# Neighbourhood attention with three units in flight, and side work placed anew, in a two-block kernel

## The chip, the cores and the metric

The kernel runs on one core of a Trainium2 chip. The metric is the device time of one execution in microseconds (us); lower is better. The core's engines run side by side, each with its own list of instructions, and wait for each other by semaphores: TensorE (PE: matrix products and transposes), VectorE (DVE), ScalarE (ACT), GpSimd (POOL), and SyncE (SP), whose queue here only starts DMA transfers. PE writes to PSUM, which has eight banks; DVE and ACT carry the results on to SBUF.

## The reference

A sequence of 512 tokens of width 1024 (and 256 context tokens) goes through two blocks. Block one has a gated linear attention layer ("A") and a dilated attention layer ("B", six heads h = 0 to 5, three groups each). Block two has two layers, l = 0 and l = 1; l = 0 updates the context too. The lines that matter, cut from `_layer`:

```python
shift, scale, gate = jnp.split((jax.nn.silu(c) @ w_mod + b_mod)[:, None, :], 3, axis=-1)
na_k, na_v, df_k, df_v, na_q, na_g, df_q, df_g, cv_a, cv_b, cv_g = _split_cols(h @ w_in, len(COL_SPLITS))
a_out = _neighbourhood_attention(...)   # 6 heads of 64: a local window with bias, and 256 context keys, one softmax
b_out = _diff_merge(_diff_attend(...))  # (softmax(q1 k1^T) - lam * softmax(q2 k2^T)) v, 4 heads; sub-layer norm weights
c_out = _conformer_conv(cv_a, cv_b, conv_w, conv_b, ln_g, ln_b)   # 31 taps over positions, LayerNorm, swish
y = jnp.concatenate([a_out * jax.nn.silu(na_g), b_out * jax.nn.silu(df_g), c_out * jax.nn.silu(cv_g)], axis=-1) @ w_out
x_new = x + gate * _rms(y, g_post)
```

## The kernel before

`schedule()` writes one list of steps. PE, DVE and ACT each walk that same list in its order and do their share of every step. A step that writes to PSUM has one job per bank, and a letter for who empties it ("a" ACT, "v" DVE); a job's `claim` on PE waits until the last job that held its bank has been emptied. An engine's instructions stay in the order of the list, so what ACT or DVE does late for one step delays all their later steps.

The projections multiply in split precision. Each weight chunk is rounded to a high part on ACT (`split hi`, L1399) and the rest is made from it on DVE (L1853) or, for early chunks, on POOL (L1303); `head_split(n)` says which. `Bproj h g` are the projections of head h in layer B, `BS`, `BT`, `BPV` its scores, transposes and products with the values, and `Bw` the weights of its three groups. For `Bw` small statistics (`stat`) go out to DRAM (`st_dram`) and back by SP's queue (L1210, L1214). Between these steps stand 16 pieces of the modulation of block two: `mod` (16 products on PE, L2403, with 1.5 MB of `w_mod` from one DMA, L1169) and `modC`, a small one behind it. SP's queue takes its transfers in order of due step, one list for all: `w_mod`, statistics, weight chunks.

In block two each layer has:

- **neighbourhood attention**, 12 units (n, j), each with two PSUM banks: `nS` (scores on PE, L2321; the maximum and bias on DVE, L2175 and L2178; exp on ACT, L1665), `nW` (DVE divides by the sum, L2187 and L1755), `nT` (eight transposes on PE, L2378, copied by ACT and by DVE, L2196) and `nPV` (product with the values, L2699, bank 6). Before, l = 0 has two units in flight (banks 0 to 3) and l = 1 three (banks 0 to 5). Between them stand the eight `gate` projections (24 products of 128x512 each) and, for l = 0, eight `gatec` (256 columns): work that PE has at hand. Each is emptied by ACT through silu (L1542, L1544), and gates 3 to 5 are then scaled on DVE by the weights of the sub-layer norm (L1755 `subw`).
- **convolution taps** (L1776, 31 for each of two feature blocks, on DVE alone), spread in portions over `nq`, the neighbourhood and the `dF k` steps; `cvT` transposes their result on PE, `cvZ` transposes back and puts it through silu on ACT (L1718).
- **differential attention**: `dF` projections, `dP`/`dX` (rope, transposes), `dv` (values), and then per item `dS` (scores; maximum on DVE L2230, exp on ACT L1703), `dT`, `dPV`.

## Time and profile before

| | |
|---|---|
| three runs | 1841.69, 1847.93, 1852.33 us; median 1847.93 |
| profiled execution | 1851.54 us, its span 1849.7 us |
| PE busy | 1692.6 us, 92% of the span |
| DVE busy | 951.9 us, 51% |
| ACT busy | 669.6 us, 36% |
| POOL busy | 221.0 us, 12% |

All times in the text are microseconds from the start of the span. A row of waits names an engine's line and what it waited for; a row of windows gives the busy time of every engine in a stretch and PEclk, the share of full TensorE clock that was granted there, which is 2.4 GHz at 1.00 and 1.2 GHz at 0.50. So PE's busy time multiplied by PEclk is what the same work takes at full clock, and a stretch less that is what waits and lower clock cost together.

### The profile page before, as it was taken

Reading aid. Unit: us, or ns where it says so; the run is one execution under the profiler, and the core shown is the slowest. Engines: PE = TensorE matmul, PEld = TensorE weight load, DVE = VectorE, ACT = ScalarE, POOL = GpSimd, SP = SyncE. Lnnn points to the kernel's source line nnn. Section 1 sums busy time; section 2 is a strip of 40 time slices with the busy share of each in tenths; the row PEclk is TensorE's granted clock in tenths of the full one; section 3 lists DMA queues with packets and bytes.
Section 4 is the critical chain, followed back from the end, with each engine's and each line's share of the span. In section 5 each row is a group of like instructions: output and inputs, shape, how many; then the busy total and the mean of one; then the engine's idle time right before and its main releaser. Section 6 shows DMA issues by size and latency. Waiting matters only on the chain.

```text
span 1849.7 us, 22824 instructions
## 1 busy us (share of the span) xinstructions
PE 1692.6 (92%) x8922; PEld 1319.2 (71%) x8922; DVE 951.9 (51%) x1662; ACT 669.6 (36%) x1249; POOL 221.0 (12%) x230
## 2 busy tenths in 40 slices
PE   7999977988999999979998899979989978987897
PEld 6866756876888888868887678845548866776553
DVE  1233263255656566465277766446654565563462
ACT  3254442333223323343215543334433245323341
POOL 3044223230000000121001100001110000000000
PEclk9998988999999999989999999979999989997699
DMA  7211042324564755333141120320012321221000
GB/s 261 69 35 58 23 182 85 103 73 115 166 173 103 171 146 141 126 114 109 42 147 41 52 69 1 118 98 1 12 44 87 120 74 52 69 91 69 1 12 35
DMA packets 170834, 161.34 MB, mean 87 GB/s; under 512 B 39958, under 2 KB 153864, under 8 KB 170696
## 3 DMA queue, kind: packets, MB, share of 16 engines
q1 hardware_dynamic: 167592, 150.04, 26.7%
q0 software_dynamic: 2848, 9.74, 1.4%
q8 instruction: 72, 1.18, 0.3%
q14 instruction: 34, 0.28, 0.1%
q10 hardware_dynamic: 288, 0.10, 0.0%
HBM read 149.80 MB, written 11.18 MB: 87 GB/s over the span
## 4 chain that ended last, share of the span: by engine, by line
PE 79%; DVE 12%; ACT 3%; issue 3%; DMA 1%; POOL 1%; ACTq 0%; SPq 0%; DVEq 0%; POOLq 0%
PE psum L2350 43%; PE psum L2321 12%; PE psum L2378 7%; PE psum L2808 6%; PE psum L2369 4%; PE psum L2479 2%; PE psum L2422 2%; DVE arena L1776 1%; DVE stat L2230 1%; PE psum L2403 1%; PE psum L2699 1%; DVE wring_r L1853 1%; DVE arena L1755 1%; DVE wring_r L1859 1%; DVE hT L1792 1%
## 5 line engine op out<-in xcount | busy, mean ns | idle before, releaser
L2350 PE MATMUL psum<-hT_r,wring_r 128*128 128x512 f32 (+1 forms) x1768 | 593.1, 394 | 0.0
L2350 PEld LDWEIGHTS psum<-hT_r,wring_r 128*128 128x128 f32 (+1 forms) x1768 | 330.8, 187 | 81.0 <-issue 8.6
L2350 PE MATMUL psum<-arena_r,wring_r 128*128 128x256 f32 (+2 forms) x1416 | 382.1, 337 | 1.8 <-DVE arena_r L1899 1.8
L1399 ACT ACTIVATE arena<-psum 128x512 f32<-128x512 f32 (+5 forms) x247 | 147.4, 620 | 504.3 <-PE psum L2350 289.2
L2321 PE MATMUL psum<-arena 128*128 128x96 f32 (+9 forms) x1460 | 240.0, 393 | 22.1 <-ACT arena L1399 11.3
L2350 PEld LDWEIGHTS psum<-arena_r,wring_r 128*128 128x128 f32 (+1 forms) x1416 | 229.0, 191 | 32.1 <-issue 4.2
L2321 PEld LDWEIGHTS psum<-arena 128*128 128x128 f32 (+5 forms) x1460 | 172.9, 205 | 85.7 <-issue 48.4
L2378 PE MATMUL psum<-ident,arena 128*128 128x128 f32 (+2 forms) x1028 | 145.4, 295 | 76.0 <-DVE arena L1755 42.7
L2350 PE MATMUL psum<-arena_r 128*128 128x512 f32 (+2 forms) x680 | 211.0, 351 | 0.0
L2378 PEld LDWEIGHTS psum<-ident,arena 128*128 128x128 f32 (+2 forms) x1028 | 126.1, 152 | 97.1 <-DVE arena L1755 47.1
L2350 PE MATMUL psum<-hT_r,arena_r 128*128 128x512 f32 (+1 forms) x408 | 163.7, 401 | 6.0 <-POOL wring_r L1303 6.0
L2350 PEld LDWEIGHTS psum<-arena_r 128*128 128x128 f32 (+1 forms) x680 | 120.9, 191 | 17.1 <-issue 0.3
L2808 PE MATMUL psum<-wring,branch 128*128 128x512 f32 x256 | 119.7, 614 | 4.9 <-issue 4.9
L1776 DVE SCALAR_TENSOR_TENSOR arena<-arena,vec 128x783 f32<-128x783 f32 (+1 forms) x120 | 108.7, 906 | 3.1
L1853 DVE SCALAR_TENSOR_TENSOR wring_r<-wring,wring_r 128x1024 fp32r<-128x1024 f32 x61 | 77.4, 1292 | 52.2 <-ACT wring_r L1399 52.0
L1399 ACT ACTIVATE wring_r<-wring 128x1024 fp32r<-128x1024 f32 (+1 forms) x87 | 88.5, 1040 | 43.2 <-DMA wring<-in_w_in 18.8
L2350 PEld LDWEIGHTS psum<-hT_r,arena_r 128*128 128x128 f32 (+1 forms) x408 | 77.8, 191 | 28.2 <-POOL wring_r L1303 6.7
L2230 DVE TENSOR_REDUCE stat<-psum 128x2 f32<-128x1536 f32 x32 | 56.2, 1757 | 80.3 <-PE psum L2321 80.3
L2808 PEld LDWEIGHTS psum<-wring,branch 128*128 128x128 f32 x256 | 47.6, 195 | 66.8 <-issue 66.8
L1399 ACT ACTIVATE arena_r<-wring 128x1024 fp32r<-128x1024 f32 (+3 forms) x74 | 77.7, 1083 | 11.9 <-DMA wring<-in_w_out 5.5
L2028 DVE LOAD_MASK_SELECT arena<-arena x18 | 0.3, 14 | 144.9 <-ACT arena L1399 144.9
L1703 ACT ACTIVATE hT<-psum,stat 128x768 f32<-128x768 f32 (+1 forms) x54 | 43.0, 802 | 73.8 <-DVE stat L1755 73.8
(221 smaller groups left out, 2059.0 us busy)
## 6 DMA issues: line engine op xcount, KB each, us to landing
wring<-in_w_in_b SPq DMA_DIRECT2D x54, 512.0 KB, 5.9
arena<-in_w_mod SPq DMA_DIRECT2D x16, 1536.0 KB, 10.1
wring<-in_w_in SPq DMA_DIRECT2D x16, 1536.0 KB, 6.9
wring<-in_w_out SPq DMA_DIRECT2D x8, 2048.0 KB, 10.8
wring<-in_w_in_a SPq DMA_DIRECT2D x5, 1536.0 KB, 6.5
arena<-x_dram SPq DMA_DIRECT2D x3, 2048.0 KB, 13.4
wring<-in_w_in SPq DMA_DIRECT2D x6, 1024.0 KB, 5.5
arena<-ebias_dram SPq DMA_DIRECT2D x144, 32.0 KB, 1.8
```

Of the source, the lines that this page charges most:

```text
L1399: return nc.scalar.activation(out, in_, ACT.Copy, scale=scale)
L1703: free(nc.scalar.activation(dst, src, ACT.Exp, bias=d_neg[:, n % 4, half:half + 1], scale=diff_scale, accum_out=d_s[:, n % 4, half:half + 1]))
L1776: ins_ = nc.vector.scalar_tensor_tensor(dst, src, w, dst, ALU.mult, ALU.add)
L1853: nc.vector.scalar_tensor_tensor(rest, w, 1.0, hi.bitcast(F32), ALU.mult, ALU.subtract).then_inc(head_lo, 1)
L2230: chained(nc.vector.reduce_max(d_max[:, p], psum[:, 0:4, 0:KEYS // 2].rearrange("p (s b) k -> p s b k", s=2), AX_XY))
L2321: ins_ = nc.tensor.matmul(out, lhsT, rhs, start=i == 0, stop=i == len(pairs) - 1)
L2350: ins_ = nc.tensor.matmul(b[0:hi.shape[2], 0:width], w[:, k], v[:, k], start=k + p == 0, stop=(k, p) == (KT - 1, 2))
L2369: ins_ = nc.tensor.matmul(out, v, w, start=i + p == 0, stop=(i, p) == (KT - 1, 2))
L2378: return nc.tensor.transpose(out, in_, ident[0:n, 0:n])
L2422: ins_ = nc.tensor.matmul(banks[g], w[:, k], v[:, k], start=k + p == 0, stop=(k, p) == (KT - 1, 2))
L2479: ins_ = nc.tensor.matmul(b[:, 0:384], v, w[:, 0:384], start=k + p == 0, stop=(k, p) == (KT - 1, 2))
L2808: ins_ = nc.tensor.matmul(psum[:, 7], src[:, k, tt * P:(tt + 1) * P], w[:, k], start=k == 0, stop=k == 5)
```

## The change

1. Modulation: no piece after `BS` of head 0, one more after `gate B 7` at the end; every piece moves one slot later. The first statistics go to SP's queue ahead of the second `w_mod`. `head_split` gives the rests of nine early weight chunks (Bproj 0) to DVE instead of POOL.
2. Neighbourhood: three units in flight in both layers. The work of DVE and ACT on the scores is a step of its own (`nM`, `nE`), placed with unit u for unit u + 2. All gates go through bank 7 (before, for l = 0, banks 4, 5 and 7). In l = 1 each gate comes in two halves (`gatep`, `gate`), one with each unit. The rounding of weights now stands behind `nE`.
3. The scaling of gates 3 to 5 is a step `subs` in the `dF k` steps. Taps: l = 0 has 6, 6, 0 in `nq` (before 5, 5, 5), l = 1 one with each unit, 12 instead of 7.
4. `cvT` stands two projections earlier; `cvZ` goes from behind `dF v 1` to behind the second `dS`; the first `dS` stands ahead of `dv`. `dv`, `cvZ` and two `dX` use banks 4 to 7 only.

```diff
@@ schedule @@
         add("aaavvvv", "BS", h)
-        modulation()
+        if h:
+            modulation()
...
             add("a", "gate", "B", 7)
+            modulation()
             add("avav", "BT", h)
...
             add(*keys[p])
+            add("", "subs", l, p)
             add("", "taps", l, ("k", p), 4 if both else 7)
...
         turn(0)
+        add("v" * (2 + both), "cvT", l)
         add(*queries[1])
         turn(1)
         add(*queries[2])
         turn(2)
-        add("v" * (2 + both), "cvT", l)
...
-        add("aa" * (1 + both), "cvZ", l)
         turn(4)
         add(*values[2])
         turn(5)
-        for t in range(TT + CT):
-            add("av"[t % 2], "dv", l, t)
-        turn(6)
-        diff_stage(add, l)
+
+        def between():
+            for t in range(TT + CT):
+                add("av"[t % 2], "dv", l, t)
+            turn(6)
+
+        def then():
+            add("aa" * (1 + both), "cvZ", l)
+
+        diff_stage(add, l, between, then)
...
@@ neighbourhood(add, l), new @@
+    filled(2)
+    for u in range(DEPTH):
+        add("aa", "nS", l, *units[u])
+        if u < 2:
+            softmax(u)
+            filled(1)
     add("", "nW", l, *units[0])
     for u, unit in enumerate(units):
+        if l == 0 and u:
+            product(u - 1)
         add("av", "nT", l, *unit)
         if u + 1 < len(units):
             add("", "nW", l, *units[u + 1])
+        softmax(u + 2)
+        if l and u:
+            product(u - 1)
+        filled(1)
+        add("", "taps", l, ("n", u), 2 - l)
+        if u + DEPTH < len(units):
+            add("aa", "nS", l, *units[u + DEPTH])
+    product(len(units) - 1)
...
@@ diff_stage @@
         if n < len(items):
             add("aa", "dS", l, *items[n])
+        if n < 2:
+            (between, then)[n]()
...
@@ banks, in hybrid_stack_kernel @@
-            free_ = (7,) if key[0] == "gate" and key[1] == "C1" else (4, 5, 7) if key[0] in ("gate", "gatec") and key[1] == "C0" else range(BANKS)
+            free_ = (7,) if key[0] in ("gate", "gatec") and key[1][0] == "C" else range(4, BANKS) if late(key) else range(BANKS)
...
         def head_split(n):
-            return n >= before_mem
+            return n >= split_at[("Bproj", 0, 0), 0]
...
-                items.append((order_of[mod_key(3 * h)] + 0.5, "stats", h))
+                items.append((order_of[mod_key(3 * h - 1) if h else ("BS", 0)] + 0.5, "stats", h))
```

In the lists below a line number of the changed kernel stands for the same operation as one about 30 lines earlier in the kernel before (L1887 for L1853, L1789 for L1755, L1810 for L1776, L2226 for L2196, L2351 for L2321, L2409 for L2378).

DVE's list before, at one unit of the neighbourhood of l = 0 (from the copy of one unit's transposes to the maximum of the next scores):

```order
L2196 COPY arena<-psum 128x512 [waits psum_full]
L1752 TENSOR_TENSOR branch<-psum,branch 128x24x16 [waits evac_scalar,psum_full]
L1853 SCALAR_TENSOR_TENSOR wring_r<-wring,wring_r 128x8x128 [waits split_hi]
L1755 TENSOR_SCALAR branch<-branch,subw 128x512 [waits evac_scalar]
L2187 RECIPROCAL stat<-stat 128x2 [waits evac_scalar]
L1755 TENSOR_SCALAR arena<-arena,stat 128x512 [waits dve_chain]
L1755 TENSOR_SCALAR arena<-arena,stat 128x512
L1776 SCALAR_TENSOR_TENSOR arena<-arena,vec 128x783
L1776 SCALAR_TENSOR_TENSOR arena<-arena,vec 128x783 [waits dve_chain]
L2175 TENSOR_REDUCE stat<-psum 128x2 [waits psum_full,bias_ready,dve_chain]
```

DVE's list of the changed kernel, at one unit of the same stage:

```order
L2226 COPY arena<-psum 128x512 [waits psum_full,dve_chain]
L2217 RECIPROCAL stat<-stat 128x2 [waits evac_scalar]
L1789 TENSOR_SCALAR arena<-arena,stat 128x512 [waits dve_chain]
L1789 TENSOR_SCALAR arena<-arena,stat 128x512
L2205 TENSOR_REDUCE stat<-psum 128x2 [waits psum_full,bias_ready]
L2208 ISA psum,stat<-psum,arena,stat 128x256 [waits dve_chain]
...
L1789 TENSOR_SCALAR stat<-stat 128x2 [waits dve_chain]
L1887 SCALAR_TENSOR_TENSOR wring_r<-wring,wring_r 128x8x128 [waits split_hi]
L1810 SCALAR_TENSOR_TENSOR arena<-arena,vec 128x783
```

The scaling by `subw`, which waited for ACT's silu, has gone from between the copy and the division; the division, the maximum and its negative follow the copy at once, and the rest of the weights (`wring_r`, which waits for `split_hi` from ACT) stands behind them where it stood ahead.

PE's list before, where the differential attention of l = 1 begins: the last transposes of `dX`, six `dv` of three products each, the first two `dS` (four rows of 128x384 products), and the transposes of `dT` (from `hT`):

```order
L2378 MATMUL psum<-ident,arena 128x128 [waits evac_scalar,diff_staged]
L2378 MATMUL psum<-ident,arena 128x128 x3
L2378 MATMUL psum<-ident,arena 128x128 [waits evac_scalar,evac_vector]
L2378 MATMUL psum<-ident,arena 128x128 x2
...
L2378 MATMUL psum<-ident,arena 128x128 [waits evac_vector,evac_scalar]
L2378 MATMUL psum<-ident,arena 128x128 x2
L2321 MATMUL psum<-arena 128x384 [waits evac_scalar,evac_vector]
L2321 MATMUL psum<-arena 128x384 x3
L2321 MATMUL psum<-arena 128x384 [waits evac_scalar]
L2321 MATMUL psum<-arena 128x384 x3
L2378 MATMUL psum<-ident,hT 128x128 [waits evac_scalar,diff_w]
L2378 MATMUL psum<-ident,hT 128x128 x5
```

PE's list of the changed kernel at the same place:

```order
L2409 MATMUL psum<-ident,arena 128x128 [waits evac_vector,diff_staged]
L2409 MATMUL psum<-ident,arena 128x128 x3
L2351 MATMUL psum<-arena 128x384 [waits evac_scalar,evac_vector]
L2351 MATMUL psum<-arena 128x384 x3
L2409 MATMUL psum<-ident,arena 128x128 [waits evac_scalar,evac_vector]
...
L2351 MATMUL psum<-arena 128x384 [waits evac_scalar]
L2351 MATMUL psum<-arena 128x384 x3
L2409 MATMUL psum<-ident,arena 128x128 [waits evac_scalar,evac_vector]
L2409 MATMUL psum<-ident,arena 128x128 x3
L2409 MATMUL psum<-ident,arena 128x128 [waits evac_vector]
L2409 MATMUL psum<-ident,arena 128x128 x3
L2409 MATMUL psum<-ident,hT 128x128 [waits evac_scalar,diff_w]
```

The first `dS` now stands ahead of the six `dv`, and the eight transposes of `cvZ` (4 and 4) between the second `dS` and the first `dT`.

SP's list before, at the end of layer B (the last chunks of w_out, then the statistics of head 5):

```order
L1161 DMA wring<-in_w_in_b 128x8x384 [waits psum_full]
L1169 DMA arena<-in_w_mod 128x8x384 [waits psum_full] x2
L1161 DMA wring<-in_w_out 128x8x512 [waits psum_full] x2
L1210 DMA st_dram<-stat 128x8x1 [waits dil_probs]
L1210 DMA st_dram<-stat 128x2x4 x2
L1214 DMA stat<-st_dram 128x2x4 [waits st_saved]
L1214 DMA stat<-st_dram 128x8x1 x2
```

SP's list of the changed kernel at the same place:

```order
L1194 DMA wring<-in_w_in_b 128x8x384 [waits psum_full]
L1202 DMA arena<-in_w_mod 128x8x384 [waits psum_full] x2
L1194 DMA wring<-in_w_out 128x8x512 [waits psum_full] x2
L1202 DMA arena<-in_w_mod 128x8x384 [waits psum_full]
L1243 DMA st_dram<-stat 128x8x1 [waits dil_probs]
L1243 DMA st_dram<-stat 128x2x4 x2
```

One transfer of `w_mod` now stands between the chunks of w_out and the statistics.

## Rows read from the trace of the kernel before

**Rows 1.** The page: PE's busy time, and the chain that ended last

```profile
PE 1692.6 (92%) x8922; PEld 1319.2 (71%) x8922; DVE 951.9 (51%) x1662; ACT 669.6 (36%) x1249; POOL 221.0 (12%) x230
...
PE 79%; DVE 12%; ACT 3%; issue 3%; DMA 1%; POOL 1%; ACTq 0%; SPq 0%; DVEq 0%; POOLq 0%
```

**Rows 2.** Waits of PE over the span: us in total, times, longest

```profile
PE psum L2378 <- DVE arena L1755: 42.7, 12, 10.3
PE psum L2378 <- DVE hT L1792: 12.4, 9, 3.5
...
PE psum L2321 <- ACT arena L1399: 11.3, 8, 2.4
...
PE psum L2321 <- ACT hT L1703: 8.0, 2, 5.5
...
PE psum L2350 <- POOL wring_r L1303: 6.0, 2, 3.6
PE psum L2403 <- issue: 5.1, 1, 5.1
```

**Rows 3.** Busy time by stretch: stretch, PE, PEld, DVE, ACT, POOL, PEclk, DMA

```profile
363.00:434.00 71.00, 65.01 (x302) 51.91 (x300) 41.31 (x55) 23.53 (x48) 18.35 (x7) 0.95 0.33 87
...
975.00:1103.00 128.00, 112.01 (x772) 91.61 (x772) 89.51 (x170) 70.07 (x109) 10.85 (x6) 0.95 0.16 46
1487.00:1600.00 113.00, 91.98 (x581) 71.79 (x581) 67.19 (x151) 57.09 (x94) 8.39 (x6) 0.89 0.21 59
...
1103.00:1186.00 83.00, 83.00 (x518) 71.85 (x515) 44.64 (x86) 27.00 (x56) 2.69 (x6) 1.00 0.20 70
1186.00:1236.00 50.00, 39.12 (x190) 27.29 (x189) 26.11 (x67) 19.45 (x53) 1.20 (x2) 0.73 0.31 116
1671.00:1746.00 75.00, 60.29 (x261) 42.28 (x260) 33.79 (x57) 25.56 (x47) 1.20 (x2) 0.64 0.12 42
```

**Rows 4.** Groups of DVE with shapes, 975:1103: busy, mean ns, idle before

```profile
L1853 DVE SCALAR_TENSOR_TENSOR wring_r<-wring,wring_r 128x1024 fp32r<-128x1024 f32 x7 | 8.6, 1225 | 10.5 <-ACT wring_r L1399 10.5
```

**Rows 5.** Timeline of a unit of l = 0: start, length, engine, idle before

```profile
1037.67 1.28 ACT L1544 ACT_TABLE_LOAD   x1
...
1038.96 0.38 ACT L1544 ACTIVATE arena<-psum 128x256 f32<-128x256 f32 x1
...
1039.38 0.35 DVE L1755 TENSOR_SCALAR arena<-arena,subw 128x256 f32<-128x256 f32 x1 [3.11 <-ACT arena L1544]
...
1040.78 1.09 PE L2378 MATMUL psum<-ident,arena 128*128 128x128 f32 x8 [1.94 <-DVE arena L1755]
```

**Rows 6.** Timeline of PE, the convolution's transposes in l = 1

```profile
1642.92 1.69 PE L2378 MATMUL psum<-ident,arena 128*128 128x128 f32 x14
1649.43 1.97 PE L2378 MATMUL psum<-ident,arena 128*128 128x128 f32 x8 [4.82 <-DVE arena L1776]
```

**Rows 7.** Timeline of DVE at the same place

```profile
1646.26 3.11 DVE L1776 SCALAR_TENSOR_TENSOR arena<-arena,vec 128x512 f32<-128x512 f32 x4
```

**Rows 8.** Timeline of POOL, rests of Bproj 0

```profile
376.59 9.03 POOL L1303 TENSOR_TENSOR wring_r<-wring,wring_r 128x1024 fp32r<-128x1024 f32 x3
```

**Rows 9.** Timelines of SP's queue and PE: w_mod transfers, modulation products

```profile
429.32 0.74 SPq L1169 DMA_DIRECT2D arena<-in_w_mod  x1
...
439.20 2.79 PE L2403 MATMUL psum<-arena,siluc 128*32 128x384 f32 x16 [5.14 <-issue]
...
766.28 1.50 PE L2403 MATMUL psum<-arena,siluc 128*32 128x384 f32 x16
```

**Rows 10.** Timelines of SP's queue and DVE, end of layer B

```profile
757.85 0.99 SPq L1161 DMA_DIRECT2D wring<-in_w_out  x2
772.15 1.51 SPq L1210 DMA_DIRECT2D st_dram<-stat  x3
...
787.02 0.17 DVE L2069 TENSOR_TENSOR stat<-stat 128x8 f32<-128x8 f32 x1 [7.05 <-DMA stat<-st_dram]
```

**Rows 11.** Timeline of ACT, silu of the convolution in l = 0

```profile
1186.52 2.36 ACT L1718 ACTIVATE arena<-psum,vec 128x512 f32<-128x512 f32 x4 [1.41 <-PE psum L2378]
```

More of the change, by code:

```diff
@@ L301, in schedule @@
                 end -= 1
-            while split < min(n + units - (key[0] in ("Bproj", "BS") or key[0] == "hcT"), end):
+            while split < min(n + units - (key[0] in ("Bproj", "BS") or key[0] == "hcT") + (key[0] == "nq") - (key[:2] == ("gate", "C1")), end):
                 out.append((("split", split), ""))
@@ L343, in neighbour_units, with product, softmax, late @@
     return [(n, j) for n in range(NQB) for j in range(NH // 2)]
[L346 to L348 removed]
 def neighbourhood(add, l):
[L354 to L356 removed]
+    units = neighbour_units()
+    gates = [step for i in range(KT) for step in ((("a", "gate", "C0", i), ("a", "gatec", "C0", i)) if l == 0 else
+                                                  (("", "gatep", "C1", i), ("a", "gate", "C1", i)))]
     def filled(n):
         for _ in range(n):
[L361 to L363 removed]
+            add(*gates.pop(0))
+    def product(u):
+        n, j = units[u]
+        add("v" * (j == NH // 2 - 1), "nPV", l, n, j)
+    def softmax(u):
+        if u < len(units):
+            add("", "nM", l, *units[u])
+            add("", "nE", l, *units[u])
+    filled(2)
+    for u in range(DEPTH):
         add("aa", "nS", l, *units[u])
[L365 removed]
+        if u < 2:
+            softmax(u)
+            filled(1)
     add("", "nW", l, *units[0])
     for u, unit in enumerate(units):
+        if l == 0 and u:
+            product(u - 1)
         add("av", "nT", l, *unit)
[L369 to L372 removed]
         if u + 1 < len(units):
             add("", "nW", l, *units[u + 1])
[L375 to L378 removed]
+        softmax(u + 2)
[6 more added lines that the diff above has]
+    product(len(units) - 1)
     assert not gates
+def late(key):
+    return key[0] == "dv" or key[0] == "cvZ" or key in (("dX", 0, "q", 2), ("dX", 0, "q", 3))
 def diff_tiles(l):
@@ L389, in diff_items, with diff_stage @@
     return [(t, h) for t in diff_tiles(l) for h in range(DH)]
-def diff_stage(add, l):
+def diff_stage(add, l, between, then):
     tiles, items = diff_tiles(l), diff_items(l)
@@ L478, in hybrid_stack_kernel @@
         readers += list(who)
-    ordinal, seen = [], {"a": 0, "v": 0}
-    for who in readers:
-        seen[who] += 1
-        ordinal.append(seen[who])
     njobs = {key: len(who) for key, who in steps}
+    ordinal, seen = [0] * len(readers), {"a": 0, "v": 0}
+    for key, _ in steps:
+        emptied = ("nS", *key[1:]) if key[0] == "nE" else key
+        if key[0] != "nS":
+            for n in range(base[emptied], base[emptied] + njobs[emptied]):
+                seen[readers[n]] += 1
+                ordinal[n] = seen[readers[n]]
     held, earlier, last_job = [], [], [-1 - i for i in reversed(range(BANKS))]
@@ L1664, in _ @@
                     for half in range(2):
-                        free(nc.scalar.activation(nprob[l][i % depth][:, half], bank(key, half), ACT.Exp,
-                                                  bias=n_neg[:, i % depth, half:half + 1],
-                                                  accum_out=n_s[:, i % depth, half:half + 1]))
+                        free(nc.scalar.activation(nprob[i % DEPTH][:, half], bank(scores, half), ACT.Exp,
+                                                  bias=n_neg[:, i % DEPTH, half:half + 1],
+                                                  accum_out=n_s[:, i % DEPTH, half:half + 1]))
                 elif kind == "nT":
@@ L2345, in split_features @@
                     evacuated(pe, ("hcT", key[1]), 3)
-                for k in range(KT):
+                for k in blocks:
                     if new and i == 0:
@@ L2426, in _ @@
                             turn_tokens(pe, ("hT", f"C{l}"), src, k + HT_BANKS)
+                elif kind == "gatep":
+                    split_features(("gate", *key[1:]), 0, 0, 0, range(KT // 2))
+                elif kind == "gate" and key[1] == "C1":
+                    split_features(key, 0, 0, 0, range(KT // 2, KT))
                 elif (split_jobs(key) and kind != "Aproj") or kind == "gatec":
```

83 lines of the change are left out of this document (33 added, 50 removed).

## The prediction, written before the changed kernel had run

> **What bounds the kernel now.** I read the page first. PE is busy for 92% of the span and makes 79% of the chain that ended last [rows 1]: the kernel goes at PE's pace, and time can come only from PE's waits and from the clock that it runs at. The waits of PE say where they are [rows 2]: 42.7 us in 12 waits for DVE's L1755, the scaling of probabilities, above all at `nT` of the neighbourhoods; then the differential attention (12.4 us for L1792, 8.0 for ACT's L1703), and single waits at rests from POOL (6.0 in two) and for w_mod (5.1). The windows by stretch give the sizes [rows 3]. In the neighbourhood of l = 0 (975 to 1103) PE is busy 112.0 of 128.0 us at a clock of 0.95: 112.0 x 0.95 = 106.4 us of work at full clock, so 21.6 are lost, 16.0 of them idle. In l = 1 (1487 to 1600) it is 92.0 of 113.0 at 0.89: 81.9 of work, 31.1 lost. In the `dF k` stretch (1103 to 1186) PE is busy all 83.0 us at 1.00 while DVE works only 44.6: DVE work is free there.
>
> The clock falls behind waits. In the stretch with no idle time it stays 1.00, in the two neighbourhoods 0.95 and 0.89, in the stretches that begin the differential attention 0.73 and 0.64 [rows 3]. The 16 modulation products that follow 5.14 us of idle took 2.79 us, the same 16 with PE busy before them 1.50 [rows 9]. A wait removed thus gives back more than itself, and I take it from these lost sums.
>
> **Part 2 and 3, neighbourhood of l = 0.** At a typical unit DVE stood 3.11 us for ACT's silu before it could scale a gate by `subw` (1039.38), the division of the probabilities came behind that, and PE waited 1.94 for it (1040.78) [rows 5]. DVE also stood 10.5 us in seven waits at a rest of the weights for ACT's high part, ahead of the division [rows 4]. The change takes both from between the copy and the division, and puts a third unit in flight, so that the softmax of u + 2 has a unit's time before `nT` needs it. What paces next? DVE is busy 89.5 us over 12 units [rows 3], 14.9 for a pair, less some 0.4 for the scalings that leave: 14.5. For PE I take 1.07 each for `nS`, `nT` and `nPV`, near the 1.09 of `nT` [rows 5], 3.2 a unit; the 16 gate pieces then have (106.4 - 38.4) / 16 = 4.25 each, and a pair of iterations, with two pieces, is 14.9. The two are level, so I allow 0.7 a pair for gates that find bank 7 not yet emptied, since ACT has two table loads of 1.28 a pair beside its exps: 15.6. Six pairs are 93.6. Ahead of the first `nT` stand four gate pieces (17.0) and three `nS` (3.2), 20.2 in all; the last three iterations have no `nS`, less 3.2. Sum 110.6, against 128.0: **-17**. From below, PE's work and nothing else (106.4) gives -21.6; from above, half of the waits stays: -11.
>
> **Part 2 and 3, l = 1.** The same with gates in halves. The tap work grows from 7 to 12, some 0.75 us each (four took 3.11) [rows 7]; DVE's 67.2 us [rows 3], less three scalings, is 10.9 a pair, 11.5 with the taps. PE's gates are (81.9 - 38.4) / 8 = 5.4, and its work of a pair 11.8. I choose 13.1 a pair, 1.3 above, for what DVE and ACT still expose: 78.6 for six. Ahead stand four half gates (10.9), and the first `nT` waits some 3.0, while DVE clears taps and a rest, with 2.5 of clock: 95.0, against 112.1 from its first to its last step: **-17**. Bounds: PE's work alone, 81.9, gives -31; half of the waits left gives -10. The lower bound is far, since here more is lost now; nearer to it I would need a pair without any wait.
>
> **Part 3 elsewhere.** The scalings, six and three operations of DVE, lie in the `dF k` steps, where DVE has 38 us to spare in l = 0 [rows 3]: 0. If that cover were gone they would cost some 2.5 us in l = 0, six at the 0.35 of a 128x256 one [rows 5] or a little more.
>
> **Part 4, cvT.** In l = 1 PE waited 4.82 us in the middle of `cvT` for the last taps, and the transposes behind it ran at a lower clock [rows 6]; DVE had four taps of 3.11 us in all still to do, behind the rope of `dP` [rows 7]. Twelve taps in the neighbourhood instead of seven make 62 of 62 done by `dF k 2`, before PE gets to `cvT`, though `cvT` stands earlier. The wait goes, 4.8, with some 2.2 of clock: **-7** (bounds -5 and -7). In l = 0 there is no such wait, before or after: 0.
>
> **Part 4, begin of the differential attention.** The first `dS` goes ahead of `dv` and starts its softmax earlier, but `dv` has only banks 4 to 7, so its fifth job waits for the copy of the first, which on ACT stands behind the exps of the first `dS`. And the silu of `cvZ`, in l = 0 2.36 us for four (1186.52) [rows 11] and one table load of 1.28 (as [rows 5] has it) each way, now stands on ACT between the second exps and the first copy of `dT`. What PE gains is that `cvZ`'s own transposes (1.3 and 0.9 us) lie under a wait. I get +2.6 - 1.3 = **+1.3** in l = 0, and **+1.4** in l = 1, at clocks of 0.73 and 0.64 [rows 3]. Bounds: all of the new order hidden, -3 each; the whole detour of ACT on the path at half clock, +5 each.
>
> **Part 1, modulation and rests.** At the start of layer B POOL took 9.03 us for three rests [rows 8], DVE takes 1.225 for one [rows 4]. PE's waits there are 6.0 in two, and the stretch 363 to 434 loses 71.0 - 65.0 x 0.95 = 9.2 us [rows 2, 3]. With DVE the first wait goes (-3.4 with its clock), a new one comes at the next projection, where the rest is queued behind DVE's copy for the projection before (1.9 taken, between nothing and the 3.4), and the wait of 3.6 shrinks to 2.4 (-1.2): -2.7. At 434 PE waited 5.14 for w_mod, issued at 429.32 and used at 439.20, and lost 6.5 with the clock [rows 9]. That wait goes; but the second w_mod is now queued behind the statistics of head 0 and, by the same 9.9 us from issue to use, comes some 2.3 us after PE gets to it: about 4.1 with clock. Net -2.4. At the end of B w_mod (1.5 MB) now lies between w_out and the statistics of head 5. Those were issued at 772.15, when the two w_out transfers had landed, and DVE had them at 787.02 after 7.05 us of idle, PE's `BT 5` waiting for it [rows 10]. In flight beside 1.5 MB the small transfers come 0.5 to 2.5 us later, and the extra `modC` pair stands between: **+2** (1 to 4). Part 1 in all: **-3**.
>
> **Sum.** -17 - 17 - 7 + 1.3 + 1.4 - 3 = -41. The profiled execution took 1851.5 us, 3.6 more than the median of the runs (1847.9). It would become 1810.5; a median over runs, 1807.
>
> **Rivals.** (a) *The chain through DVE and ACT paces on.* With one bank for all gates, each gate waits for ACT, which stands in exps and table loads. ACT works 70.1 us in l = 0 [rows 3], 5.8 a unit, and can't reorder. Then half of the neighbourhoods' loss stays: 1824. For it: DVE's 14.5 a pair is level with PE's 14.9. Against: both have slack of some 40 and 60 us in the stage before. Chance 0.2. The Trainium skill (ScalarE: Activation LUTs, What ACT_TABLE_LOAD costs) gives 1.28 us for the load and 1.38 more for a drain, 2.66 a switch. By that, an estimate, two switches a unit would add 2.8 us to each of ACT's units and bring case (a) about in l = 0. Here the load took 1.28 and the next activation began 1038.96, where the load ended [rows 5]; the drain is not seen, and it adds nothing to the chance.
> (b) *Slower.* Bank 7 makes the stage serial: a gate can't start until ACT has emptied the one before, ACT stands behind the exps of u + 2, these behind DVE's maximum, and that behind the scores which PE issues after the gate. A unit of l = 0 would be about 14.7 us (gate and gatec on average 4.3, `nS` and `nPV` 2.1, division, `nT`, copy, maximum, exps, silu with its loads 8.3) for 10.7 now, 48 us for twelve, with half of that in l = 1: 1890. It turns the sign from 13.4 a unit on. Against: the scores of u + 2 are issued a unit ahead. Chance 0.04, with 0.05 more that losses and gains cancel within 0.5%.
> (c) *More is gained.* PE has hardly a wait left, the clock stays at 1.00 in both neighbourhoods as it does in the `dF k` stretch, and the pairs go at PE's work, 106 and 87: 1793. Chance 0.11.
> (d) *The begin of the differential attention costs more*, 4 to 5 us a layer: 1814, inside my own range.
>
> **How the numbers follow.** The forecast with (d) has 0.6, its own range 1796 to 1818. (a) 0.2, (c) 0.11, no change 0.05, slower 0.04. Leaving out a tenth at either side, the range is 1790 to 1829. 0.5% is 9 us, about what a measurement of this kernel tells from no change: faster 0.91, same 0.05, slower 0.04.
>
> **What the profile after would show.** Right: PE's waits for L1755 (now L1789) fall from 42.7 to below 20; windows of the two neighbourhoods of about 111 and 95 us at a clock of 0.97 and more; no wait at `cvT` in l = 1; no wait of PE for POOL in B; one wait for w_mod at the second piece, smaller than 5.1. Wrong: PE waits at gates for ACT's silu, or for L1399 at `nS`; the first `dT` in either layer waits more than before; or the statistics of head 5 reach DVE more than 19 us after their issue (now 14.9).

## The result, and the profile after

The changed kernel takes 1829.11 us (median of four runs, 1826.59 to 1830.79) against 1848.14 of the kernel before (four runs); the ratio is 0.990, 95% interval 0.987 to 0.993. It is faster by 19 us where I had forecast 41, and the time lies 0.1 us above the range.

The page of the changed kernel, its busy times and the chain that ended last (before: [rows 1]):

```profile
PE 1685.2 (92%) x8922; PEld 1309.9 (72%) x8922; DVE 950.4 (52%) x1671; ACT 672.8 (37%) x1251; POOL 195.0 (11%) x221
...
PE 78%; DVE 11%; ACT 4%; issue 4%; DMA 1%; POOL 1%; ACTq 0%; DVEq 0%; POOLq 0%
```

Waits of PE over its span: us in total, times, longest (before: [rows 2]):

```profile
PE psum L2434 <- issue: 19.0, 7, 8.9
PE psum L2409 <- DVE arena L1789: 17.9, 3, 10.3
...
PE psum L2409 <- ACT arena L1752: 9.9, 2, 5.4
PE psum L2380 <- ACT branch L1575: 7.3, 6, 2.2
...
PE psum L2409 <- ACT arena L1432: 6.8, 2, 4.4
PE psum L2380 <- ACT arena L1577: 6.6, 6, 1.9
```

What was aimed at has gone: the waits for the scaling of probabilities fell from 42.7 us in 12 to 17.9 in 3 (two of the three, 15.1 us of it, lie outside the windows of the two neighbourhoods), and the waits for `hT` by the first `dS` of the differential attention (8.0) and for the last taps are no more in the list. Four new ones stand in their place: L2434, the modulation's products, which wait for w_mod seven times (19.0, before 5.1 in one); L1575 and L1577, silu of the gates in bank 7; L1752, silu of `cvZ`; and a copy by L1432 for `dv`.

The windows of the two neighbourhoods, each from its first step to its last, changed kernel (columns as in [rows 3]):

```profile
979.90:1096.70 116.80, 107.97 (x770) 88.67 (x770) 78.56 (x158) 71.54 (x109) 8.66 (x6) 0.99 0.18 51
1484.00:1581.70 97.70, 88.37 (x578) 67.04 (x576) 65.81 (x150) 53.58 (x91) 7.69 (x6) 0.95 0.22 61
```

and the same two stretches of the kernel before:

```profile
974.90:1102.80 127.90, 111.91 (x770) 91.53 (x772) 89.41 (x169) 70.07 (x109) 10.85 (x6) 0.95 0.16 46
1487.20:1599.20 112.00, 91.00 (x577) 71.14 (x577) 66.38 (x148) 57.09 (x94) 8.39 (x6) 0.89 0.20 56
```

l = 0 went from 127.9 to 116.8 and l = 1 from 112.0 to 97.7: -11.1 and -14.3, and the clock rose in both. To see the rest I laid the starts of PE's steps of both traces side by side; how much a stretch between two steps grew or shrank is its part:

| stretch of PE's steps | forecast | measured |
|---|---|---|
| ahead of layer B (untouched by the change) | 0 | -2.9 |
| start of layer B: Bproj 0 and the first two w_mod | -5.1 | -4.7 |
| heads 1 to 5 of layer B | 0 | +10.7 |
| its end, gate B 5 to the hT transposes of l = 0 | +2 | +2.0 |
| neighbourhood, l = 0 | -17 | -11.1 |
| `cvT` to the third tile of the differential attention, l = 0 | +1.3 | +2.9 |
| neighbourhood, l = 1 | -17 | -14.3 |
| `cvT` in l = 1 | -7 | -5.9 |
| from there to the third tile | +1.4 | +2.7 |
| sum | -41.4 | -20.6 (the spans differ by 20.8) |

The largest surprise is 10.7 us in the heads of layer B, 8.7 of them in head 3 alone.

Some of these parts vary from trace to trace without any edit. What stands ahead of layer B took 357.7 to 363.2 us in the twelve traces that can be read, so the -2.9 is no gain of the change. The stretch from `BS` of head 0 to `BS` of head 1 took 66.4 us in the changed kernel and 63.6 to 65.0 in the eight other kernels that place the pieces as it does, so the -4.7 is on the low side.

### The profile page after: what moved, and what is told of

Its sections match the earlier page's. It is cut to its first block, busy times and chain, and to the rows that moved or that the text cites. A ratio compares the mean times of both kernels' runs of the same rounds, so it can differ in the third digit from the quotient of the medians.

```text
span 1828.9 us, 22822 instructions
## 1 busy us (share of the span) xinstructions
PE 1685.2 (92%) x8922; PEld 1309.9 (72%) x8922; DVE 950.4 (52%) x1671; ACT 672.8 (37%) x1251; POOL 195.0 (11%) x221
## 4 chain that ended last, share of the span: by engine, by line
PE 78%; DVE 11%; ACT 4%; issue 4%; DMA 1%; POOL 1%; ACTq 0%; DVEq 0%; POOLq 0%
PE psum L2380 44%; PE psum L2351 11%; PE psum L2843 7%; PE psum L2409 6%; PE psum L2400 4%; PE psum L2514 2%; PE psum L2453 2%; PE psum L2434 1%; DVE stat L2260 1%; DVE arena L1810 1%; DVE wring_r L1887 1%; DVE arena L1789 1%; DVE wring_r L1893 1%; ACT arena L1699 1%; DVE psum L2208 1%
## 5 line engine op out<-in xcount | busy, mean ns | idle before, releaser
L1432 ACT ACTIVATE arena<-psum 128x512 f32<-128x512 f32 (+5 forms) x247 | 147.2, 619 | 479.4 <-PE psum L2380 254.6
L2351 PE MATMUL psum<-arena 128*128 128x96 f32 (+9 forms) x1460 | 235.7, 387 | 4.6 <-ACT arena L1432 2.2
L2351 PEld LDWEIGHTS psum<-arena 128*128 128x128 f32 (+5 forms) x1460 | 169.1, 201 | 68.2 <-issue 46.2
L2409 PE MATMUL psum<-ident,arena 128*128 128x128 f32 (+2 forms) x1028 | 143.5, 292 | 48.0 <-DVE arena L1789 17.9
L2409 PEld LDWEIGHTS psum<-ident,arena 128*128 128x128 f32 (+2 forms) x1028 | 124.3, 151 | 68.8 <-issue 20.1
L1887 DVE SCALAR_TENSOR_TENSOR wring_r<-wring,wring_r 128x1024 fp32r<-128x1024 f32 x68 | 85.1, 1278 | 76.7 <-ACT wring_r L1432 76.5
L1432 ACT ACTIVATE wring_r<-wring 128x1024 fp32r<-128x1024 f32 (+1 forms) x87 | 88.3, 1039 | 56.2 <-DMA wring<-in_w_in 19.2
L1810 DVE SCALAR_TENSOR_TENSOR arena<-arena,vec 128x783 f32<-128x783 f32 (+1 forms) x120 | 106.9, 891 | 2.9
L2380 PEld LDWEIGHTS psum<-hT_r,arena_r 128*128 128x128 f32 (+1 forms) x408 | 77.1, 189 | 30.7 <-issue 7.6
L1432 ACT ACTIVATE arena_r<-wring 128x1024 fp32r<-128x1024 f32 (+3 forms) x74 | 77.7, 1082 | 16.9 <-DMA wring<-in_w_in_b 6.2
L1887 DVE SCALAR_TENSOR_TENSOR wring_r<-wring,arena_r 128x1024 fp32r<-128x1024 f32 x49 | 62.7, 1302 | 14.0 <-ACT arena_r L1432 13.8
## 6 DMA issues: line engine op xcount, KB each, us to landing
arena<-x_dram SPq DMA_DIRECT2D x3, 2048.0 KB, 10.6
```

What stands on the lines that cost most here:

```text
L1432: return nc.scalar.activation(out, in_, ACT.Copy, scale=scale)
L1810: ins_ = nc.vector.scalar_tensor_tensor(dst, src, w, dst, ALU.mult, ALU.add)
L1887: nc.vector.scalar_tensor_tensor(rest, w, 1.0, hi.bitcast(F32), ALU.mult, ALU.subtract).then_inc(head_lo, 1)
L2351: ins_ = nc.tensor.matmul(out, lhsT, rhs, start=i == 0, stop=i == len(pairs) - 1)
L2380: ins_ = nc.tensor.matmul(b[0:hi.shape[2], 0:width], w[:, k], v[:, k], start=k + p == 0, stop=(k, p) == (KT - 1, 2))
L2409: return nc.tensor.transpose(out, in_, ident[0:n, 0:n])
```

## The experiments

Each kernel ran four times, except those of experiments 4 and 5 (once). "Less than the changed kernel" compares medians with 1829.11 us. The kernel before was timed anew beside each group of runs: 1848.62 us beside experiments 1, 2, 3 and 7, 1849.68 beside 6, 8, 9 and 11, 1848.56 beside 4, 5 and 10, against 1848.14 above. So such a difference is good to some 1.5 us, beside the spread of the runs themselves.

**1. `modT` later.** In head 3 of the changed kernel PE waits twice for w_mod (L2434). SP's queue there, then POOL's and two rows of PE:

```profile
622.91 12.51 SPq L1210 DMA_DIRECT2D ebias_dram<-rpb_dram  x16
635.46 0.45 SPq L1202 DMA_DIRECT2D arena<-in_w_mod  x1
636.26 10.31 SPq L1243 DMA_DIRECT2D st_dram<-stat  x3
658.40 1.50 SPq L1247 DMA_DIRECT2D stat<-st_dram  x3
659.94 2.74 SPq L1194 DMA_DIRECT2D wring<-in_w_in_b  x3
662.73 2.12 SPq L1202 DMA_DIRECT2D arena<-in_w_mod  x1
...
631.00 1.88 POOL L1322 DMA_DIRECT2D gate_dram<-stat  x2 [293.09 <-DVE stat L1786]
...
649.39 1.50 PE L2434 MATMUL psum<-arena,siluc 128*32 128x384 f32 x16 [1.31 <-issue]
...
672.84 2.79 PE L2434 MATMUL psum<-arena,siluc 128*32 128x384 f32 x16 [4.85 <-issue]
```

The same queue in the kernel before, and `modT`'s two transfers at 611.56, ahead of the head's bias writes (`ebias_dram`), w_mod and statistics:

```profile
629.72 12.26 SPq L1177 DMA_DIRECT2D ebias_dram<-rpb_dram  x16
642.32 0.38 SPq L1169 DMA_DIRECT2D arena<-in_w_mod  x1
642.76 3.92 SPq L1210 DMA_DIRECT2D st_dram<-stat  x3
657.76 2.17 SPq L1214 DMA_DIRECT2D stat<-st_dram  x3
659.98 2.92 SPq L1161 DMA_DIRECT2D wring<-in_w_in_b  x3
662.94 1.60 SPq L1169 DMA_DIRECT2D arena<-in_w_mod  x1
...
611.56 1.89 POOL L1289 DMA_DIRECT2D gate_dram<-stat  x2 [199.50 <-DVE stat L1752]
```

The statistics went out and were ready to be read back 15.0 us later (642.76 to 657.76); in the changed kernel it took 22.1 (636.26 to 658.40), and the next w_mod stands behind that. Most of the difference arises while SP still issues the three writes: 10.31 us instead of 3.92. The edit:

```diff
-            if j == MODS - 1:
-                add("", "modT", l)
+            if (l, j) in ((1, 1), (1, MODS - 1)):
+                add("", "modT", 0 if j == 1 else 1)
```

> The changed kernel with one step moved: `modT` of layer 0, which sends the modulation's gate vector to DRAM by two small transfers from POOL, stands two pieces later, behind the second modulation piece after it. Theory 1 (the small scattered writes at 631 us share the DMA engines with the bias writes, w_mod and the statistics of head 3, and hold w_mod up): PE's waits of 1.3 and 4.9 us for w_mod in head 3 go, the piece of layer B from BS 3 to BS 4 takes 65.2 us as before the change instead of 73.8, and the kernel 8 to 9 us less: about 1820.5. Theory 2 (SP's queue itself is too late, since PE now reaches the pieces some 7 us earlier against the bias writes that stand ahead of w_mod on it): the waits stay, time 1829 within 3.

Measured: 1818.52 us, 0.983 of before (0.981 to 0.985), 10.6 less than the changed kernel. Its SP queue and the window of head 3:

```profile
632.78 0.45 SPq L1202 DMA_DIRECT2D arena<-in_w_mod  x1
633.59 3.80 SPq L1243 DMA_DIRECT2D st_dram<-stat  x3
648.33 1.50 SPq L1247 DMA_DIRECT2D stat<-st_dram  x3
```

```profile
621.70:687.10 65.40, 65.22 (x365) 53.51 (x364) 38.49 (x78) 21.22 (x46) 1.88 (x2) 1.00 0.62 149
```

14.7 us from the writes to the reads, a head of 65.4 us instead of 73.8, and the clock at 1.00. SP's queue stands to PE as it did: w_mod is issued 11.1 us after the start of `BS 3` in both. The rival (a queue that is late by itself) falls, and of theory 1 so much is shown: the two writes delay the transfers beside them. That they do it in the DMA engines is not shown. All traces agree: with `modT` where the change put it, head 3 takes 71.4 to 73.8 us (five kernels), otherwise 65.2 to 66.3 (seven).

The gain fell 22 us short, and this step is the largest single part of that: 10.6 us by the medians, 8.4 in head 3 by the traces. Another 4.9 us by which this trace is shorter in layer B lie in the heads before and behind, which the edit doesn't reach.

**2. Modulation undone.**

```diff
-        if h:
-            modulation()
+        modulation()
...
             add("a", "gate", "B", 7)
-            modulation()
...
-                items.append((order_of[mod_key(3 * h - 1) if h else ("BS", 0)] + 0.5, "stats", h))
+                items.append((order_of[mod_key(3 * h)] + 0.5, "stats", h))
```

> The changed kernel with the modulation pieces and the statistics on SP's queue put back where they were before the change; POOL's nine rests stay on DVE. If the new places cost what the two traces show (head 3 +8.7 us, small waits in heads 2 and 4 +2, end of layer B +2, against -5 for the first piece), the kernel takes some 8 us less than the changed one: about 1821. If the placement is as good as I predicted (-0.4 net without the rests), it takes the same time, 1829, or a little more.

Measured: 1824.28 us, ratio 0.987 (0.985 to 0.989); 4.8 less than the changed kernel. That is between the two expectations (8 and 0). From layer B's start to the hT transposes of l = 0 its trace takes 0.6 us more than the kernel before, the changed kernel 7.9 more. So the new places cost as built, and the collision is the reason: with `modT` out of the way (experiment 1) the same places take 5.0 us less than before.

**3. Begin of the differential attention undone.**

```diff
         add(*values[1])
+        add("aa" * (1 + both), "cvZ", l)
         turn(4)
         add(*values[2])
         turn(5)
-        def between(): ...
-        def then(): ...
-        diff_stage(add, l, between, then)
+        for t in range(TT + CT):
+            add("av"[t % 2], "dv", l, t)
+        turn(6)
+        diff_stage(add, l)
```

> The changed kernel with the begin of the differential attention put back: `cvZ` behind the second value projection, `dv` and the last `dX` ahead of the first `dS`, all banks free to them. `cvT` stays early. My theory (`dv 4` waits in bank 4 for ACT's copy of `dv 0`, which stands behind the exps of the first `dS`, and the first `dT` for cvZ's silu): it takes 5.6 us less than the changed kernel (2.9 in l = 0, 2.7 in l = 1), about 1823.5. Rival (the half clock after this place has its own causes, and the new order costs nothing): 1829 within 2.

Measured: 1818.85 us, ratio 0.984 (0.981 to 0.986), 10.3 less than the changed kernel. By the stretches of the traces 3.3 us are of l = 0 and 3.9 of l = 1; the rest is of other places, above all of layer B, where this run's waits for w_mod were shorter (4.8 us), which the edit does not touch. My mechanism had two parts, so three more kernels take them apart. All are read in us from the start of `dF v 1` to the first `dS` of a later tile, `dS 0 0 0` in l = 0 and `dS 1 2 0` in l = 1, so that `cvZ`'s place is inside for all:

| kernel | l = 0 | l = 1 |
|---|---|---|
| before | 59.4 | 87.6 |
| changed | 62.4 | 91.5 |
| 3. begin undone | 59.1 | 87.6 |
| 4. only `cvZ` moved | 64.4 | 91.0 |
| 5. only `dv` moved | 58.4 | 87.8 |
| 6. `dv` readers exchanged | 62.0 | 89.7 |

This stretch varies too: the kernels of experiments 1 and 2, which are as the changed kernel here, took 62.7 and 64.2 us in l = 0 and 91.5 and 91.4 in l = 1; those of experiments 8 to 11, which are as kernel 3, took 59.2 to 60.3 and 85.5 to 88.7. So kernels of the same order differ by up to 3 us. Over all twelve traces those with `cvZ` moved lie at 61.9 to 64.4 and 89.6 to 91.5, the others at 58.4 to 60.3 and 85.5 to 88.7, and the groups don't overlap.

**4. Only `cvZ` moved,** with `dv` and two `dX` still in banks 4 to 7.

```diff
-        diff_stage(add, l, between, then)
+        between()
+        diff_stage(add, l, lambda: None, then)
```

> The changed kernel with `dv` and the last `dX` put back ahead of the first `dS`, while `cvZ` stays behind the second. Read from the start of `dF v 2` to the first `dS` of the next tile that runs at full clock (`dS 0 0 0` and `dS 1 2 0`), where the changed kernel took 52.5 and 81.6 us, diff_start_undone 47.9 and 76.9. If cvZ's silu on ACT ahead of the first `dT` is the larger part, most of the 4.6 and 4.7 us stays: 51 to 53 and 80 to 82. If `dv` behind the softmax is, 48 to 50 and 77 to 79.

**5. Only `dv` moved.**

```diff
         add(*values[1])
+        add("aa" * (1 + both), "cvZ", l)
...
         def then():
-            add("aa" * (1 + both), "cvZ", l)
+            pass
```

> The changed kernel with `cvZ` put back behind `dF v 1`, while the first `dS` stays ahead of `dv` and `dv` keeps banks 4 to 7. The same stretches. If `dv` behind the softmax costs time, they stay above 47.9 and 76.9 by 1 us or more; if issuing the first `dS` early is worth its 2 us and only cvZ's silu cost, they fall below these, to 46 and 75.

One run each: 1831.26 and 1822.59 us. The expectations counted the stretch from `dF v 2`: 54.6 and 81.1 us for only_cvz_moved, 47.2 and 77.1 for only_dv_moved. With `cvZ` moved the loss stays whole; with `dv` moved neither of the two cases came, the times are those of kernel 3. So `cvZ` behind the second `dS` makes the loss, and for the first `dS` ahead of `dv` neither gain nor loss is seen: 0.7 us less than kernel 3 in l = 0, 0.2 more in l = 1. PE in l = 1, only `cvZ` moved:

```profile
1666.93 2.93 PE L2352 MATMUL psum<-arena 48*128 48x384 f32 x8 [5.48 <-ACT hT L1738]
1669.79 1.78 PE L2410 MATMUL psum<-ident,arena 128*128 128x128 f32 x8
1676.80 1.51 PE L2410 MATMUL psum<-ident,hT 128*128 128x128 f32 x6 [5.23 <-ACT arena L1753]
```

only `dv` moved:

```profile
1660.59 1.51 PE L2410 MATMUL psum<-ident,arena 128*128 128x128 f32 x6 [4.40 <-ACT arena L1433]
1662.03 2.93 PE L2352 MATMUL psum<-arena 48*128 48x384 f32 x8
1668.50 1.54 PE L2410 MATMUL psum<-ident,hT 128*128 128x128 f32 x6 [3.54 <-DVE hT L1827]
```

With `dv` moved, the softmax of the first item is waited for at `dv 4` (4.40) where it was waited for at the second `dS` (5.48 above): the same wait, 1.1 us smaller, at another step. With `cvZ` moved, the first `dT` waits 5.23 for its silu and not 3.54 for the combined weights. ACT of the changed kernel at that place:

```profile
1671.55 0.90 ACT L1737 ACTIVATE hT<-psum,stat 128x768 f32<-128x768 f32 x1 [5.51 <-DVE stat L1789]
...
1673.44 1.28 ACT L1752 ACT_TABLE_LOAD   x1
1674.74 1.45 ACT L1752 ACTIVATE arena<-psum,vec 128x512 f32<-128x512 f32 x2
```

The silu of `cvZ` starts only after both exps and a table load and ends at 1676.2; the first `dT` takes bank 4, which it holds, at 1676.33.

**6. The readers of `dv` exchanged.**

```diff
-                add("av"[t % 2], "dv", l, t)
+                add("va"[t % 2], "dv", l, t)
...
-                elif kind == "dv" and key[2] % 2 == 0:
+                elif kind == "dv" and key[2] % 2:
```

> The changed kernel with the readers of the six `dv` banks exchanged: DVE copies the first, third and fifth, ACT the others. `dv 4` then waits in bank 4 for DVE's copy and not for ACT's, but DVE has the maximum of the first `dS` (1.8 us each in l = 1) ahead of it, and `dv 5` in bank 5 still waits for ACT behind the exps. Theory (a copy in bank 4 or 5 that stands behind the softmax on its engine is what holds PE): the wait moves from `dv 4` to `dv 5` and the time stays within 2 us of 1829. Rival (only ACT's copy of `dv 0` matters): 4 us in l = 1 and 2 in l = 0 go.

Measured: 1827.49 us, ratio 0.987 (0.985 to 0.989), 1.6 less than the changed kernel. PE waited 1.2 us at `dv 4` (DVE) and 2.6 at `dv 5` (ACT) in l = 1 instead of 4.4 at `dv 4`: the wait moved as the theory says.

**7. Silu ahead of the exps.**

```diff
-        softmax(u + 2)
         if l and u:
             product(u - 1)
         filled(1)
+        softmax(u + 2)
```

> The changed kernel with each gate's step of the neighbourhood ahead of the softmax steps of unit u + 2, so that ACT empties bank 7 before it does these exps. Theory: the waits of PE for silu in bank 7 (6.6 us in six in l = 0, 6.5 in five in l = 1) go, with their share of clock, and the kernel takes 8 to 14 us less: about 1818. Rival: the exps now wait for the gate's last product, and with them the `nT` of u + 2; then waits of `nT` for DVE come back and the time stays at 1829 or rises.

Measured: 1807.68 us (median of the three runs of 1805 to 1809), ratio 0.978 (0.976 to 0.980), 21.4 less than the changed kernel where 8 to 14 were expected. The fourth run, the one with the trace, took 5763 us, PE's products being some three times as long from start to end; why is not known. It is left out, and the next kernel shows the stage.

**8. Three edits together** (1, 3 and 7).

> The changed kernel with the three edits together: `modT` of layer 0 later, the begin of the differential attention as it was before the change, and the silu of the gates ahead of the exps. If each took its time from a place of its own, as the stages of the traces say (head 3 -8.4 us, the two begins -7.1, the two neighbourhoods what is left of the 21 us by which silu_before_exps was faster than the changed kernel), they add: about 1791, between 1787 and 1797. If the edits give the same time twice (SP's queue late again once PE is earlier), it stays above 1800. The neighbourhoods should show no wait of PE for silu in bank 7 and a clock of 1.00, which the single run of silu_before_exps left without a readable profile.

Measured: 1800.02 us, ratio 0.973 (0.971 to 0.975). The neighbourhoods from `gate C0 0` to the last `nPV`, and from `gate C1 0` to the last `nPV` of l = 1:

```profile
973.00:1080.80 107.80, 105.29 (x771) 87.40 (x770) 81.33 (x158) 70.95 (x109) 7.95 (x6) 1.00 0.19 55
1466.30:1554.30 88.00, 85.22 (x578) 65.00 (x576) 66.30 (x150) 56.33 (x93) 7.66 (x6) 0.98 0.23 68
```

and all waits of PE in the first and in the second of the two (L2371 is the line of the gate products, L2400 that of the transposes):

```profile
PE psum L2371 <- DVE arena L1780: 1.5, 1, 1.5
PE psum L2371 <- ACT branch L1566: 0.8, 1, 0.8
PE psum L2371 <- ACT arena L1568: 0.2, 1, 0.2
...
PE psum L2400 <- DVE arena L1780: 2.8, 1, 2.8
```

l = 0 takes 107.8 us instead of 116.8, l = 1 88.0 instead of 97.7. The exps, now later by a gate, hold nobody up. So each neighbourhood had 9 us left in ACT's order, in waits and in the clock behind them, and the rival of experiment 7 falls. The sum came out 9 us above my 1791: PE's waits for w_mod are back, 14.5 us in four with 10.2 at the end of layer B, and the layer takes 6.6 us more than in experiment 1. That part of the gain is given back there, in a layer that the other two edits don't touch.

**9. The last piece late.**

```diff
             add("a", "gate", "B", 5)
-            add("", "Bw", h)
-            modulation()
             add("a", "gate", "B", 6)
             add("a", "gate", "B", 7)
+            add("", "Bw", h)
             modulation()
             add("avav", "BT", h)
...
+        if h == BH - 1:
+            modulation()
         add("va", "BPV", h)
```

> The same as three_edits, with the end of layer B changed: the last w_mod is needed only after `gate B 7` (order: gate B 5, 6, 7, Bw, piece, `BT`, piece, `BPV`). Theory: PE's 8.9 us wait for w_mod behind the w_out transfers lies under two gates of 5.4 us, and the statistics of head 5, which come in the same microseconds, are hidden too: 5 to 7 us less than three_edits. Rival: w_mod and the statistics land together at the end of the gates, `BT 5` waits for the statistics instead, and nothing is gained (within 2).

Measured: 1796.34 us, ratio 0.971 (0.969 to 0.974), 3.7 less than three_edits on the same chip; the two intervals overlap, so by the times alone this gain is not certain. The queue and PE at the end of layer B:

```profile
760.29 0.37 SPq L1194 DMA_DIRECT2D arena<-in_w_mod  x1
764.61 1.62 SPq L1235 DMA_DIRECT2D st_dram<-stat  x3
777.37 1.50 SPq L1239 DMA_DIRECT2D stat<-st_dram  x3
...
777.27 1.50 PE L2426 MATMUL psum<-arena,siluc 128*32 128x384 f32 x16
785.05 3.17 PE L2401 MATMUL psum<-ident,arena 128*128 128x128 f32 x15 [6.28 <-DVE arena L1778]
```

The products wait no more for w_mod; `BT 5` waits 6.28 us for the statistics, as it did before the change. By the stage of the traces (`gate B 5` to `BPV 5`: 35.1 us in three_edits, 29.2 here) it saves 5.9 us, so the theory holds in its first half; that the statistics would be hidden too was wrong.

**10. Rests back on POOL,** in the kernel of 9.

```diff
-            return n >= split_at[("Bproj", 0, 0), 0]
+            return n >= before_mem
```

> The kernel of late_end_piece with the nine rests of Bproj 0 back on POOL. By the stages of seven traces the rests on DVE save 2.8 us at the first projection, cost 3.9 at the second and save 1.2 at the third, so nothing: 1796 within 2. By my prediction (-3.4, +1.9, -1.2) it is 2.7 us slower, about 1799.

Measured: 1792.56 us, ratio 0.970 (0.967 to 0.972). The intervals of 9 and 10 overlap, so the two can't be told apart; 2.7 us slower it is not. Against the kernel before, Bproj 0 is 1.6 us shorter in this trace, with the rests on the same engine; with DVE its three projections are -2.8, +3.9 and -1.2. Over all traces the engine makes no difference: from the first projection to `BS` of head 0 it is 64.5 to 66.1 us with POOL (three kernels) and 64.5 to 66.2 with DVE (nine).

**11. The neighbourhood alone.** The changed kernel with the edits of 2, 3 and 10, and

```diff
         turn(0)
-        add("v" * (2 + both), "cvT", l)
         add(*queries[1])
         turn(1)
         add(*queries[2])
         turn(2)
+        add("v" * (2 + both), "cvT", l)
```

> The kernel before with the neighbourhood part of the change alone (three units in flight, softmax and gates placed anew, taps and the sub-layer scaling moved); modulation, POOL's rests, `cvT`, `cvZ`, `dv` and the first `dS` are where they were. From the stages of the traces: -11 to -13 us in l = 0, -14 to -16 in l = 1, and part of the 5.9 at `cvT` (its last taps come earlier now) though `cvT` stands late: about 1817 to 1823 against 1848, so faster than the whole change. If the parts help each other, it is slower than the whole change, above 1829.

Measured: 1816.55 us, ratio 0.982 (0.980 to 0.984), 12.6 us faster than the whole change, so the parts don't help each other. -10.4 in l = 0, -14.5 in l = 1, and the full -5.9 at `cvT`, where it stood before: five more taps in the neighbourhood are enough, and the earlier place of `cvT` gives nothing.

## Why the prediction was wrong

**The sign and the places of the gain were right; two terms of the sum were not:** layer B (-3 forecast, +8.0 measured) and the neighbourhoods (-34 forecast, -25.4 measured). What the forecast says of the removed waits for L1755 was borne out: they fell below 20 us. The clock of 0.97 and more came in l = 0 (0.99), not in l = 1 (0.95). Of the signs that would show the forecast wrong two came: gates waited for ACT's silu, and the first `dT` waited longer (5.42 us for 3.51 in l = 1). The third did not: the statistics of head 5 reached DVE 15.3 us after their issue.

**Part 1, modulation: the step that failed.** I followed the pieces on SP's queue and PE at the two ends of layer B, and put heads 1 to 5 at nothing, without a reason but that every piece moves one slot later. They cost 10.7 us, 8.7 in head 3. What moved there with the piece was `modT`, whose two small writes from POOL went from 611 into the microseconds of bias writes, w_mod and statistics. Experiment 1 takes them out, and head 3 is back at 65.4; the other 2 us in the heads are waits for w_mod that differ from trace to trace. All transfers of a moved step count, those of POOL too; POOL's timeline of the kernel before has them at 611. And the slack was small: before, the w_mod issued at 662.94 took 9.7 us, and PE needed it at 673.04, 0.4 later.

**Part 1, its ends.** Start -4.7 for -5.1 was right by luck: the rests brought 0 where I had -2.7, as the new wait at the second projection costs 3.9 and not the 1.9 that I chose, with its clock. The first w_mod brought -6.7 for -6.5 and the second cost 4.0 for 4.1; the missing 2.1 are the pair of `mod` and `modC` that leaves this place for the end of the layer, which I counted only there. At the end +2.0 for +2 was luck as well: I kept `BT 5`'s wait and let the statistics come 0.5 to 2.5 us later, a term that no row shows; from issue to DVE they took 15.3 us for 14.9. What came instead was a wait of PE for w_mod of 8.89 us, and `BT 5`'s wait, 8.1 us with its clock, disappeared behind it. That w_mod took 15.0 us to land (770.82 to 785.79). The w_out transfers, which the expectation of experiment 9 blames, had landed at 775.3; from 780 to 784 the DMA engines moved nothing (last section), and it landed among the statistics' writes (782.6 to 786.8). Why it took so long is open.

**Neighbourhood, l = 0.** The pair of iterations was sized right: from the third `nT` (1017.88) to the eleventh (1080.39) there are four pairs of 15.6 us. The 6 us are at the ends: all ahead of the first `nT` took 23.0 us instead of 20.2, since the first two gate pieces wait (1.5 us for DVE, 0.8 for the silu in bank 7), and the last pair took 16.3, no shorter without `nS`, as `gate C0 7` waited 1.9 for silu and then ran at a clock of 0.76. **Rival (a)** described this: gates wait for ACT in bank 7, behind exps. Its condition, that half of the neighbourhoods' loss stays, came true: 21.6 and 31.1 us were lost, and 25.4 were gained. The waits are as it says, 6.6 us in six in l = 0 and 6.5 in five in l = 1; the prediction put them at 0.7 a pair and gave the rival 0.2. It also counted two table loads a pair, where ACT has four (25 in this window, before 23). Experiment 8 shows 9 us in each layer. It was not that ACT is short of time: it works 71 us in 8 as in the changed kernel and has 25 table loads there too. It was the order of its list. The Trainium skill's drain of 1.38 us behind a table load (ScalarE: Activation LUTs, What ACT_TABLE_LOAD costs) is not seen here either: at 1673.44 the load takes 1.28 and the activation starts at 1674.74.

**l = 1 and cvT.** -14.3 for -17 and -5.9 for -7: right mechanisms, the wait of the first `nT` 2.78 us for 3.0; what is missing are the gates that waited.

**Begin of the differential attention.** The mechanism was there, both waits came at the steps named, but the sum of +2.7 was half of the 5.6 measured. What was named first (`dv 4`) has a wait but no cost of its own; the silu of `cvZ` is what costs (experiments 4 and 5).

Rivals (b) and (c) fell. (c)'s 1793 was reached by kernel 10, and in part by what it says: windows of 107.8 and 88.0 us at a clock of 1.00 and 0.98, which kernel 8 shows. Three figures of the rivals and bounds don't follow from their terms: half of the 52.7 us lost would make (a) about 1815 (1824 is half of the forecast gain), (b)'s 1890 leaves out its own half for l = 1 (with it about 1913, and the sign turns at 11.1 us a unit), and the bound of -10 in l = 1 is half of the idle time, while -11 in l = 0 is half of the loss. None of them enters the sum.

What stays open is why the waits for w_mod in heads 1, 2 and 4 lie between 0 and 2.4 us from trace to trace with the same order, which also blurs the additions of experiments 2, 3 and 8, and what in the two small writes holds the other transfers up.

## What to carry to other kernels

When a step is moved, list every transfer that it issues, on every queue, and look up what already flows in the microseconds it is moved into; a step "one slot later" need not be free where a single buffer is refilled just in time. When waits on one engine are taken away, look at the order in which the next engine empties PSUM: work that frees a bank for the bottleneck goes ahead of work that is needed a unit later. Try the parts of a change apart; here one part alone was faster than all four, and three small corrections of the rest took it from 1829 to 1800 us.

## What the runs showed of the hardware that was not expected

Two transfers of 4 KB each from POOL, 64 packets in all, made the way of three statistics transfers to DRAM 7 us longer (22.1 for 15.0). Of this 6.4 us passed while SP issued the three: 10.31 us for 3.92, 9.3 to 10.4 in all five kernels with the writes there and 3.5 to 4.0 in the seven others. The w_mod transfer of 1.5 MB in flight beside them grew as well. Its landing time in the kernel before at 609.81 (POOL's writes beside it, at 611.56) and at 642.32 (no writes of POOL), and in the changed kernel at 635.46 (writes at 631.00):

```profile
arena<-in_w_mod SPq DMA_DIRECT2D x1, 1536.0 KB, 16.5
arena<-in_w_mod SPq DMA_DIRECT2D x1, 1536.0 KB, 10.2
arena<-in_w_mod SPq DMA_DIRECT2D x1, 1536.0 KB, 13.8
```

In experiment 1 the w_mod at 632.78 took 9.4 us and the one at 665.89, beside the writes at 667.40, 16.6. So the writes cost the same sort of time before the change and after its correction; only there nobody waited for that w_mod, which PE needed 26 us after its issue in the kernel before. The size of a transfer says little of what it costs others, and whether that matters is decided by the slack of what flies beside it.

Bandwidth was not all that was short. While the w_mod of 609.81 was still to land (at 626.3), and while that at the end of layer B in the changed kernel was (at 785.79), the engines moved next to nothing for some microseconds:

```profile
618.00:620.00 2.00, 2.00 (x10) 1.65 (x10) 0.00 (x0) 0.00 (x0) 0.00 (x0) 1.00 0.18 4
780.00:784.00 4.00, 0.00 (x0) 0.00 (x0) 2.87 (x1) 2.08 (x3) 1.79 (x1) 0.53 0.00 0
```

(kernel before, changed kernel; the last two columns are the DMA share and GB/s). In both, small writes to DRAM were in flight beside w_mod. What holds the transfers up meanwhile, no run here separates.
